# The odd mixer's first products as three products of split operands, the gate's product in PSUM, and new seams in the expert layers

## The reference

```python
# a sub-layer: h = x * (1 + scale) + shift;  x = layer_norm(ALPHA * x + gate * f(h), ln_g, ln_b)

def _odd_mixer(u, w_in, conv_w, conv_b, dt_bias, a_log, d_skip, norm_w, w_out, h_st):
    z, xbc, dt = jnp.split(u @ w_in, [D_INNER, D_INNER + CONV_DIM], axis=-1)   # 2048, 3072, 64 columns
    xbc = lax.conv_general_dilated(xbc, conv_w[:, None, :], ..., feature_group_count=CONV_DIM)   # 5 taps
    xbc = jax.nn.silu(xbc + conv_b)
    ...
    y = y.reshape(bsz, t, D_INNER) * jax.nn.silu(z)
    y = y * lax.rsqrt(jnp.square(y).mean(-1, keepdims=True) + 1e-5) * norm_w
    return y @ w_out, fin

def _peer(x, w_q, sub_keys, u_tab, v_tab):                 # 16384 experts, 8 heads, 16 chosen in each
    q = (xb @ w_q).reshape(PEER_BLOCK, H_P, 2, D_HALF)
    ...
    act = jax.nn.gelu(jnp.einsum('thkd,td->thk', u_tab[idx], xb), approximate=False)
    return jnp.einsum('thk,thkd->td', g * act, v_tab[idx])
```

## Time and profile before

| | |
|---|---|
| median of 3 runs | 5290.85 us (5290.58 to 5291.23) |
| the profiled execution | 5291.39 us, its span 5289.6 us |
| mean granted clock of TensorE | 0.966 of full speed |
| busy PE | 4958.3 us, 94% of the span, 25991 instructions |
| busy PEld | 4138.8 us, 78% |
| busy DVE | 3122.6 us, 59%, 4995 instructions |
| busy ACT | 1453.2 us, 27%, 1836 instructions |
| busy POOL | 1493.5 us, 28%, 839 instructions |
| DMA | 838.02 MB, mean 158 GB/s |

### The profile page before, as it was taken

How to read it: one execution, slowest core, us unless ns; L and a number is a source line. 1 busy time by engine, 2 the same in 40 slices (tenths; PEclk the granted TensorE clock), 3 DMA queues, 4 the chain that set the end, 5 groups by cost and what they waited for, 6 DMA issues and landing times.

```text
span 5289.6 us, 62573 instructions
## 1 busy us (share of the span) xinstructions
PE 4958.3 (94%) x25991; PEld 4138.8 (78%) x25991; DVE 3122.6 (59%) x4995; ACT 1453.2 (27%) x1836; POOL 1493.5 (28%) x839
## 2 busy tenths in 40 slices
PE   5979879999999989999799999899999999899997
PEld 3757778888888878888566679888888888788886
DVE  2160679918886266666555541389738883366666
ACT  0121122224444222222222222112234443222222
POOL 0030222332232365541111100123332323555531
PEclk8989989999999999999799999899999999999999
DMA  7150022334555578885200011113335554688873
GB/s 303 66 218 32 21 88 98 118 128 159 179 167 179 208 277 299 300 300 200 95 33 32 33 44 40 49 57 112 128 119 180 167 174 161 233 305 299 299 298 139
DMA packets 281036, 838.02 MB, mean 158 GB/s; under 512 B 25078, under 2 KB 163574, under 8 KB 220334
## 3 DMA queue, kind: packets, MB, share of 16 engines
q1 hardware_dynamic: 67104, 520.91, 26.1%
q10 hardware_dynamic: 168592, 178.71, 10.3%
q0 software_dynamic: 45056, 134.38, 7.4%
HBM read 677.02 MB, written 156.82 MB: 158 GB/s over the span
## 4 chain that ended last, share of the span: by engine, by line
PE 88%; DVE 6%; POOL 2%; DMA 2%; ACT 1%; issue 1%; SPq 0%; DVEq 0%; ACTq 0%; POOLq 0%
PE PS L604 21%; PE PS L605 21%; PE PS L606 21%; PE PS L753 3%; PE PS L452 3%; PE PS L866 3%; PE PS L844 3%; PE PS L512 3%; PE PS L673 2%; PE PS L828 2%; POOL A L1973 1%; PE PS L596 1%; DVE EP L1427 1%; DMA ring<-in_w_mod 1%; PE PS L750 1%
## 5 line engine op out<-in xcount | busy, mean ns | idle before, releaser
L1961 POOL TENSOR_TENSOR wL<-raw,wH 128x2048 fp32r<-128x2048 f32 x144 | 668.3, 4642 | 1540.7 <-ACT wH L1682 1540.7
L604 PE MATMUL PS<-hH,wH 128*128 128x512 f32 (+1 forms) x2560 | 964.4, 377 | 29.7 <-DVE hL L1181 28.6
L605 PE MATMUL PS<-hL,wH 128*128 128x512 f32 (+1 forms) x2560 | 960.7, 375 | 0.0
L606 PE MATMUL PS<-hH,wL 128*128 128x512 f32 (+1 forms) x2560 | 959.6, 375 | 0.0
L1682 ACT ACTIVATE wH<-raw 128x2048 fp32r<-128x2048 f32 x272 | 520.6, 1915 | 1053.4 <-PE PS L606 1044.8
L606 PE MATMUL PS<-wH,WL 128*128 128x512 f32 x2048 | 801.9, 392 | 0.0
L604 PEld LDWEIGHTS PS<-hH,wH 128*128 128x128 f32 x2560 | 484.0, 189 | 101.4 <-issue 29.4
L1302 DVE TENSOR_TENSOR wL<-raw,wH 128x2048 fp32r<-128x2048 f32 x128 | 293.3, 2292 | 451.6 <-ACT wH L1682 451.6
L606 PEld LDWEIGHTS PS<-hH,wL 128*128 128x128 f32 x2560 | 483.0, 189 | 82.9
L605 PEld LDWEIGHTS PS<-hL,wH 128*128 128x128 f32 x2560 | 483.8, 189 | 69.4
L1981 POOL DMA_INDIRECT ubuf<-in_v,idxV x256 | 359.2, 1403 | 578.2 <-DVE acc L1314 534.1
(11 more groups left out here) (349 smaller groups left out, 7994.4 us busy)
## 6 DMA issues: line engine op xcount, KB each, us to landing
raw<-in_u SPq DMA_DIRECT2D x128, 1024.0 KB, 6.1
raw<-in_v SPq DMA_DIRECT2D x128, 1024.0 KB, 4.9
expert_acts<-abuf ACTq DMA_DIRECT2D x128, 512.0 KB, 3.2
expert_gates<-wide ACTq DMA_DIRECT2D x64, 1024.0 KB, 6.5
wide<-expert_acts SPq DMA_DIRECT2D x64, 1024.0 KB, 5.9
ring<-in_w_mod SPq DMA_DIRECT2D x48, 1024.0 KB, 9.7
wide<-expert_gates SPq DMA_DIRECT2D x16, 2048.0 KB, 11.7
gb<-expert_gates SPq DMA_DIRECT2D x16, 2048.0 KB, 11.2
```

The costliest lines, as they stand in the source:

```text
L604: nc.tensor.matmul(out, lhsH, rhsH, start=start, stop=False)
L605: nc.tensor.matmul(out, lhsH, rhsL, start=False, stop=False)
L606: return nc.tensor.matmul(out, lhsL, rhsH, start=False, stop=stop)
L1961: G.tensor_tensor(wL[:, n % NSPLIT, :], raw[:, n % NRAW, :], wH[:, n % NSPLIT, :].bitcast(f32), ALU.subtract).then_inc(lo_u, 1)
```

## The change

Dt, the convolution's projections and z become split products. While they run, three slots of the ring (0 to 2) hold raw weight slices; over the other five lie oH, the high half of h for all tokens, and two buffers oHi for the high half of a slice. The low half of a slice is written over the raw one (oLo), the low half of h over hT (oL). ACT makes the high halves (weight_high, tile_high), DVE the low ones (weight_low, tile_low): slices 0 and 1 and the tiles of h at the start, the others one behind every second step of the convolution and one in every slice of z. The projections go by halves of 320 tokens, so ACT fills the padded rows by three copies. A slot is loaded when the products of the slice in it are done; slots 3 to 7 get their slices of w_oout after the last product of z. PE awaits dt's operands tile by tile.

In the normalisations the gate's product stays in PSUM (or acc0), and the sum reads it there; the buffers of PSUM come free one operation later. The factor is made before the tile ahead is scaled. In the expert layers the additions run one round later, in groups of 16 gathered activations; the wait for stored activations and the load of gates move behind ACT's second round; the first half of the first query waits for three tiles of h instead of five.

```diff
...
+    ringR = sb("ringR", [P, NSLOT * KD * SLICE], f32r, scope=rx)
+    oL = sb("oL", [P, KD, T], f32r, scope=rx)
+    rx.close()
+    W = KD * SLICE
+    oH = ringR[:, 3 * W:3 * W + KD * T].rearrange("p (k t) -> p k t", k=KD)
+    oHi = [ringR[:, 3 * W + KD * T + i * W:3 * W + KD * T + (i + 1) * W] for i in range(2)]
+    oLo = [ringR[:, i * W:(i + 1) * W] for i in range(3)]
...
+            def take_split(j, src):
+
+                uses[j % 3] += 1
+                split_use[j], split_width[j] = uses[j % 3], src.shape[-1]
+                pe.wait_ge(lo_w, j + 1)
+                slices.append([src, None, j % 3, None])
+                return [z[:, 0:src.shape[-1]].rearrange("p (k n) -> p k n", k=KD) for z in (oHi[j % 2], oLo[j % 3])]
...
-            def feature_major_split(slot, m, pair):
+            def feature_major_split(slot, m, pair, split=None):
                 for half in range(2):
+                    if split is not None:
+                        pe.wait_ge(hl_ready, split + (3 if half == 0 else NT))
...
                 modulated(2)
-                w = take(a["w_dt"]).rearrange("p (k n) -> p k n", k=KD)
+                wh, wl = take_split(0, a["w_dt"])
                 for t in range(NT):
+                    pe.wait_ge(hs_ready, t + 1)
+                    tt = slice(t * P, (t + 1) * P)
                     for k in range(KD):
-                        last = nc.tensor.matmul(PS[:, 0, t * 64:(t + 1) * 64], hT[:, k, t * P:(t + 1) * P], w[:, k, 0:64],
-                                                start=(k == 0), stop=(k == KD - 1))
+                        last = split_products(PS[:, 0, t * 64:(t + 1) * 64], oH[:, k, tt], oL[:, k, tt], wh[:, k, 0:64], wl[:, k, 0:64],
+                                              k == 0, k == KD - 1)
...
-                                w = take(a["w_xbc"][g, m // 2]).rearrange("p (k n) -> p k n", k=KD)
+                                wh, wl = take_split(1 + g * 3 + m // 2, a["w_xbc"][g, m // 2])
...
+                            for half in range(2):
+                                c = slice(half * HT, (half + 1) * HT)
+                                for k in range(KD):
+                                    last = split_products(PS[:, b + half, 0:HT], wh[:, k, mc], wl[:, k, mc], oH[:, k, c], oL[:, k, c],
+                                                          k == 0, k == KD - 1)
...
-                ws = [take(a["w_oout"][s]).rearrange("p (k n) -> p k n", k=2 * KD) for s in range(KD)]
+                ws = [take(a["w_oout"][s], s, ("z", D_INNER // SLICE - 1, NT - 1)).rearrange("p (k n) -> p k n", k=2 * KD) for s in range(KD)]
...
+            def tile_low(t):
+
+                tt = slice(t * P, (t + 1) * P)
+                ve.wait_ge(hs_hi, t + 1)
+                V.tensor_tensor(oL[:, :, tt], hT[:, :, tt], oH[:, :, tt].bitcast(f32), ALU.subtract).then_inc(hs_ready, 1)
...
+                ve.wait_ge(hi_w, j + 1)
+                V.tensor_tensor(oLo[j % 3][:, 0:w], ring[:, j % 3, 0:w], oHi[j % 2][:, 0:w].bitcast(f32), ALU.subtract).then_inc(lo_w, 1)
...
                 for t in range(NT):
+                    if n == 2 and t:
+                        tile_low(t - 1)
                     ve.wait_ge(products, at["h", n, t])
...
-                        gated(i)
-                        link(V.scalar_tensor_tensor(x[:, i, :], x[:, i, :], ALPHA, f[:, i, :], ALU.mult, ALU.add))
+                        part, evac, count = gated(i)
+                        V.scalar_tensor_tensor(halves(x[:, i, :]), halves(x[:, i, :]), ALPHA, part, ALU.mult, ALU.add).then_inc(evac, 1)
+                        ve.wait_ge(evac, count)
...
+                        ve.wait_ge(dev_ready, 2 + n * NT + i + 1)
+                        link(V.reciprocal(rstd[:, i:i + 1], rstd[:, i:i + 1]))
+                        V.scalar_tensor_tensor(nmr[:, i:i + 1], mv[:, i, 0:1], -1.0, rstd[:, i:i + 1], ALU.mult, ALU.mult).then_inc(ln_factors, 1)
                     t = i - 1
...
-                    if k % 32 == 0:
-                        c = slice(k, k + 32)
-                        ve.wait_ge(a0_full[k // 32], 16 * 32 * (l + 1))
+                    if k % 16 == 0:
+                        c = slice(k, k + 16)
+                        ve.wait_ge(a0_full[k // 16], 16 * 16 * (l + 1))
...
-                    before, share = min(HK, max(0, 9 * (hs - 2) // 2)), min(HK, max(0, 9 * (hs - 1) // 2))
+                    before, share = min(HK, max(0, 9 * (hs - 3) // 2)), min(HK, max(0, 9 * (hs - 2) // 2))
...
             def odd():
+                weight_low(0)
+                weight_low(1)
                 modulated(2)
+                tile_low(NT - 1)
...
+                        if m % 2 == 0 and m < 6:
+                            weight_low(2 + g * 3 + m // 2)
...
+                act.wait_ge(h_evac_v, at_h[2] + t + 1)
+                act.wait_ge(h_evac_a, at_h[2] + t + 1)
+                S.activation(oH[:, :, tt], hT[:, :, tt], ACT.Copy).then_inc(hs_hi, 1)
...
+                act.wait_ge(slot_full[j % 3], 16 * split_use[j])
+                if j >= 2:
+                    act.wait_ge(products, at[split_label[j - 2]])
+                S.activation(oHi[j % 2][:, 0:w], ring[:, j % 3, 0:w], ACT.Copy).then_inc(hi_w, 1)
...
-                for half in range(2):
-                    act.wait_ge(a_stored[half], 16 * 32 * (l + 1))
-                load_gates(2 * l + 1, gate_rows)
                 for hs in range(32):
+                    if hs == 2:
+                        for half in range(2):
+                            act.wait_ge(a_stored[half], 16 * 32 * (l + 1))
+                        load_gates(2 * l + 1, gate_rows)
...
-                    load(src, None)
-                    freed.append(at[entry[1]])
+                    slot, after = entry[2], entry[3]
+                    if slot in freed:
+                        sp.wait_ge(products, freed[slot])
+                    if after is not None and slot >= 3:
+                        sp.wait_ge(products, at[after])
+                    sp.dma_start(ring[:, slot, 0:src.shape[-1]], src).then_inc(slot_full[slot], 16)
+                    freed[slot] = at[entry[1]]
...
```

More of the change, by code:

```diff
@@ L316, in trunk @@
     gat_full = [sem(f"gat_full{i}") for i in range(NGAT)]
-    a0_full = [sem(f"a0_full{i}") for i in range(4)]
+    a0_full = [sem(f"a0_full{i}") for i in range(8)]
     ab_full, gb_full = [sem("ab_full0"), sem("ab_full1")], [sem("gb_full0"), sem("gb_full1")]
@@ L381, in done, with take, release_split @@
                 at[label] = state["n"]
-            def take(src):
-                n = state["slice"]
-                state["slice"] += 1
-                pe.wait_ge(slot_full[n % NSLOT], 16 * (n // NSLOT + 1))
-                slices.append([src, None])
-                return ring[:, n % NSLOT, 0:src.shape[-1]]
+            def take(src, slot=None, after=None):
+                if slot is None:
+                    slot = state["slice"] % NSLOT
+                    state["slice"] += 1
+                uses[slot] += 1
+                pe.wait_ge(slot_full[slot], 16 * uses[slot])
+                slices.append([src, None, slot, after])
+                return ring[:, slot, 0:src.shape[-1]]
+            def take_split(j, src):
[4 more added lines that the diff above has]
+                return [z[:, 0:src.shape[-1]].rearrange("p (k n) -> p k n", k=KD) for z in (oHi[j % 2], oLo[j % 3])]
             def release(label):
                 slices[-1][1] = label
+            def release_split(j, label):
+                slices[-1][1] = label
+                split_label[j] = label
             def evacuated(kind, fam, m):
@@ L748, in odd @@
                             b = 2 * (m % 2)
-                            for k in range(KD):
-                                nc.tensor.matmul(PS[:, b, 0:P], w[:, k, (m % 2) * P:(m % 2 + 1) * P], hT[:, k, 0:P],
-                                                 start=(k == 0), stop=(k == KD - 1))
-                            for k in range(KD):
-                                last = nc.tensor.matmul(PS[:, b + 1, :], w[:, k, (m % 2) * P:(m % 2 + 1) * P], hT[:, k, P:T],
-                                                        start=(k == 0), stop=(k == KD - 1))
+                            mc = slice((m % 2) * P, (m % 2 + 1) * P)
+                            for half in range(2):
[3 more added lines that the diff above has]
+                                                          k == 0, k == KD - 1)
                             done(last, ("xbc", g, m))
                             if m % 2 == 1:
-                                release(("xbc", g, m))
+                                release_split(1 + g * 3 + m // 2, ("xbc", g, m))
                         mm = m - 1
@@ L837, in odd @@
                 for s in range(D_INNER // SLICE):
-                    w = take(a["w_z"][s]).rearrange("p (k n) -> p k n", k=KD)
+                    wh, wl = take_split(13 + s, a["w_z"][s])
                     for t in range(NT):
```

(20 more changed lines are left out.)

58 lines of the change are left out of this document (37 added, 21 removed).

## The result

The changed kernel takes 5226.75 us (median of 4 runs, 5224.11 to 5230.24) against 5291.04 before (median of 4): a ratio of 0.9877, 95% interval 0.9864 to 0.9889. The forecast was 5221, range 5202 to 5250.

A forecast was written before the change was run, and what follows sets the result against it. TensorE (PE), busy 94% of the span, was taken as the bound. Terms -38 - 23 + 12 + 8.5 + 6 - 31 + 0 - 4 = -69.5 us gave 5221 against the median of 5290.85; range 5202 to 5250.

The forecast's parts named there:

- Convolution and z: Odd mixer's projections and z: split products take less PE time than f32 ones, -38 and -23 us.
- no gain in the products: Rival, 4%: three split products cost what f32's two instructions do; 61 us of gain missing, 5282.
- the splits do not fit: Rival, 13%: in the convolution, DVE misses every second step by 1.3 us or ACT's order costs as much; +16, 5237.
- slower: Rival, 4%: with three slots PE stands 9.1 us before each of 20 slices; +182, 5403.
- Start of the mixer: Before dt: weight slices and h tiles are split with DVE and ACT awaiting each other, 3.63 us a tile; +12.
- dt: Step products: 120 split products replace 80 instructions at the same 0.217 us, set by the weight load; +8.5.
- rival of cheap narrow products: Rival, 12%: dt's narrow products cost one pass of weights, or get a faster clock; -13, 5208.
- End of the mixer: After z: six w_oout loads start together, PE stands 4.9 us and about 1 for slower clock; +6 (0 to +8).
- Seam: Expert layer's passage to its values: additions one round later remove PE's 27.8 us of waits and slow clock; -31.
- rival of the moved wait: Rival, 7%: additions wait one round later as before, since row gathers come late; 28 to 31 us stay, 5251.
- Normalisations: Earlier factor shortens tiles and tail, later additions delay the expert layers' start by 5.4 us; 0 for both.
- Queries: First query asks for three tiles of h first, 1.3 us earlier; with the tail, twice 2.0: -4.

The follow-up runs named there:

- the first two runs: Changed kernel with the additions again one round earlier: 5247.65 us; changed kernel with groups of 32 gathered activations put back: 5227.52 us.
- the run with the old pace: Changed kernel with the expert additions again beginning one round earlier, still in groups of 16 activations: 5247.65 us, +20.9.
- dt's extra passes: Changed kernel with three more passes of dt's 120 split products, 32, 64 and 128 columns wide, into an unread bank: 5302.96 us, +76.2.
- the ring undone: Changed kernel with DVE's low half of each h tile behind its next tile, and weight slice 1's halves behind the last tile: 5216.44 us, -10.3.
- dt the other way round: Changed kernel with four further edits together, plus dt's weight slice stationary and h moving in two halves of 320 tokens: 5182.13 us, ratio 0.9795.

## Why the prediction was right, and where it was off

*Convolution and z.* Right in mechanism and size: 7.60 a step against 7.58 forecast, 117.0 for z against 117. That the splits would fit "with nothing to spare" was nearly so: at eight slices PE went on only behind DVE's low half, and this cost about 1.7 us where 1 was charged. The rivals "no gain in the products", "the splits do not fit" (+16) and "slower" (+182) fell.

*Start of the mixer.* +12.1 against +12, a tile in 3.63 us as forecast, and the ring is the main cause: undoing DVE's order takes 5.9 of the 12 away, moving slice 1 another 2.2.

*dt.* +8.5 as forecast, and half of the reason is shown: the width does nothing from 32 to 128 columns. That it is the weight load which sets the 0.2133 is argued from the records of PEld only. The rival of cheap narrow products fell. By the Trainium skill's page "TensorE: Matmul & The Clock Gate", section "LDWEIGHTS (loading the stationary operand)", dt would have come to an estimated 12.8; the trace does not agree, since by the 107 ns of that section for a load half of the 213 ns of a product would be left, which no number of columns explains.

*End of the mixer.* +6.8 against +6. The six loads took 19.1 us from the last z product (3196.24 to 3215.30) and not 17.4, so PE stood 6.6 longer, not 4.9; the slow clock behind it cost 0.2, not 1.

*Seam.* -30.8 against -31, by the delay alone, as the first two runs show. The rival of the moved wait fell. One step of the argument was wrong and did no harm: I held that POOL's gathers would not move, since they do not depend on DVE. The values begin at 1802.62 before and 1803.93 after; the second row's addition starts 65.8 us behind that before and 70.6 after. In the run with the old pace, where DVE stands idle for 21.69 us ahead of the first row, it is 65.5 (1863.45 from 1797.97). Most fetches take 0.94 us, but those that lie across the change from one of DVE's subtractions to its next operation, and the one behind each, take 1.9 to 2.4; ten of the 32 are slow here and six in the two kernels with the old pace. POOL's timeline at two of them:

```profile
1818.29 2.12 POOL L2051 DMA_INDIRECT A<-prompt_acts,idxA  x1 [0.30 <-issue]
1820.72 1.89 POOL L2051 DMA_INDIRECT A<-prompt_acts,idxA  x1 [0.30 <-issue]
```

So the low half came at 1878, not 1873, and of the 7 us that I had between it and PE 3.1 were left (2.2 two blocks later in the second expert layer, the least of all). Had I needed them, the term would have failed; that they were there was luck, since I had not asked what a busy DVE does to POOL.

*Normalisations.* Forecast 0, measured -0.2 up to the last normalised tile, and both halves of the sum are shown: +5.8 and +5.6 up to the last normalised tile when the factor meets POOL again (5.7 forecast), -5.4 and -5.6 when the additions begin a round earlier (5.4 forecast). The Trainium skill's page "SBUF — State Buffer", section "SBUF: two separate sides", has the lock that fits the 2328 ns; the run with the factor moved agrees, and shows that PSUM operands alone do not take it away.

*Queries.* -3.7 against -4.

*What had no term.* The scans' +3.1 by the clock, and +1.0 at the end. These two, the 0.8 of the end of the mixer and the 0.3 of the queries make 5.2 of the 5.75 between 5221 and 5226.75.

The scans' loss is no price of the new products as such. In the runs with dt's extra passes and with the ring undone, which have the same projections and scans, the scans take 4.6 us less in all than in the changed kernel and the projections 3.4 more. The clock at their starts differs: the third group's scans and the second group's projections with the ring undone, then the second group's projections in the changed kernel:

```profile
2872.90:2878.90 6.00, 6.00 (x38) 5.68 (x39) 0.00 (x0) 3.43 (x10) 5.82 (x6) 0.76 0.01 3
2695.75:2701.75 6.00, 6.00 (x23) 6.00 (x24) 0.00 (x0) 0.00 (x0) 0.00 (x0) 0.51 0.01 3
...
2710.19:2716.19 6.00, 6.00 (x29) 6.00 (x30) 0.00 (x0) 0.00 (x0) 0.00 (x0) 0.67 0.01 3
```

Why the clock is granted later now at the one and now at the other is open.

At the end the last tile is normalised 21.9 us behind the last value (22.2 before), but from there to the end of the span it is 5.8 us where it was 4.5. The stores do not set this: the packets of the last one end 2.3 us behind its issue, at 5224.96 (3.7 before), and the span ends at 5228.5. The end follows POOL's closing DRAIN, an instruction that the traces record from the start of POOL's last addition on, with 10.3 us in all twelve profiled runs; here it ends at 5228.24. The last tile is now normalised 4.7 us behind that start and no longer 6.2, so more of the 10.3 is left. With the factor late it is 6.2 again, and 4.5 to the end. What POOL does in these 10.3 us the traces do not show.

*The range.* One sum of the prediction does not come out: the low ends that it names for dt, the end of the mixer and two tails make 5200, not 5202. Nothing hangs on it here.

## What to carry to other kernels

A term of zero that is made of a gain and a loss deserves an experiment on each half: here it hid two gains of some 12 us, of which the change took only one. When an operation is split for a cheaper product, look at who prepares the operands at the first use: a ring between two engines cost some 6 us that a change of order took away, and narrow products paid a fixed price each until the operands changed places. A burst of loads that must wait for one event is hidden if the consumer asks for the pieces one by one.

## What the runs showed of the hardware that I had not expected

- Split products with 32, 64 and 128 moving columns cost the same 0.2133 us at the 1.2 GHz level.
- TensorE worked without a gap for 102 us on such products (2545.13 to 2647.60) and was granted 0.50 throughout. With dt the other way round the first 5.0 us had a mean of 0.58 and the next 5.0 us 1.00.
- The issue of POOL's gathers takes 1.9 to 2.4 us instead of 0.94 beside some of DVE's operations; with ten slow ones instead of six among the 32 fetches ahead of the first row that made 4.6 us, 67.6 instead of 63.0 from the start of the values to the landing of the first row.
- POOL's closing DRAIN is recorded with 10.3 us from the start of POOL's last addition in all twelve profiled runs, and the span ends 0.2 to 0.4 us behind it, though the last store's packets end 3.3 us earlier in the changed kernel and 0.4 earlier in the one before.
